# Router of a mixture-of-experts stage: fed from unscaled half rows, choices by the eight largest values, one load issued earlier

## The reference, cut to what matters

```python
h = x + merged @ w_out                         # 544 x 1024
xn = rms_norm(h, norm2_g)                      # h * rsqrt(mean(h*h) + EPS) * norm2_g
group_probs = softmax(xn @ w_group)            # 4 groups
gp, gi = top_k(group_probs, 1)
elog = (xn @ w_router).reshape(-1, 4, 8)       # 32 experts, 8 in each group
elog = take_along_axis(elog, gi)               # the 8 of the chosen group
ev, ei = top_k(elog, 2)
ew = softmax(ev) * gp
y = h + sum over the two chosen experts e of  ew * (silu(xn @ w_gate[e]) * (xn @ w_up[e])) @ w_down[e]
```

## Time and profile before

| | |
|---|---|
| median of 3 runs | 912.67 us (912.48 to 913.17) |
| profiled execution, device time | 908.81 us |
| its span, first to last instruction | 907.0 us |
| mean granted TensorE clock | 0.961 |
| PE busy | 822.3 us (91%) |
| DVE / ACT / POOL busy | 324.1 / 222.8 / 164.6 us |
| DMA, whole span | 164.65 MB, mean 182 GB/s |
| the chain that ended last, by engine | PE 72%, SP's queue 10%, DMA 6%, DVE 4% |

### The profile page before, as it was taken

How to read it: one execution, slowest core, us unless ns; L and a number is a source line. 1 busy time by engine, 2 the same in 40 slices (tenths; PEclk the granted TensorE clock), 3 DMA queues, 4 the chain that set the end, 5 groups by cost and what they waited for, 6 DMA issues and landing times.

```text
span 907.0 us, 11366 instructions
## 1 busy us (share of the span) xinstructions
PE 822.3 (91%) x4409; PEld 504.9 (56%) x4409; DVE 324.1 (36%) x882; ACT 222.8 (25%) x457; POOL 164.6 (18%) x225
## 2 busy tenths in 40 slices
PE   5989999999999989999999999996799999887860
PEld 3465444588665765676666684555455555454530
DVE  4222655998443531122222273545400000000005
ACT  3021332112333333333333430112122221111110
POOL 2323440000332222100000001100233232222110
PEclk9999999999999999999999999997799999999995
DMA  8523020421200200303021198217899999999968
GB/s 277 158 94 119 7 94 1 144 75 70 93 1 1 93 2 0 100 1 140 1 54 41 65 414 349 93 48 285 320 413 415 413 400 387 396 394 380 390 239 295
DMA packets 53159, 164.65 MB, mean 182 GB/s; under 512 B 13445, under 2 KB 15717, under 8 KB 44369
## 3 DMA queue, kind: packets, MB, share of 16 engines
q1 hardware_dynamic: 46432, 149.86, 43.9%
q0 software_dynamic: 6672, 14.06, 4.1%
HBM read 153.65 MB, written 18.08 MB: 189 GB/s over the span
## 4 chain that ended last, share of the span: by engine, by line
PE 72%; SPq 10%; DMA 6%; DVE 4%; POOL 3%; ACT 3%; issue 2%; POOLq 0%; DVEq 0%; ACTq 0%
PE quad L789 25%; PE pair L1120 9%; SPq L698 6%; PE pair L983 5%; PE quad L1339 4%; SPq L694 4%; PE pair L1339 4%; PE quad L857 3%; DMA arena<-in_w_up 3%; PE pair L1350 2%; PE pair L779 2%; PE quad L1077 2%; PE quad L1350 2%; POOL arena L1768 2%; PE pair L904 1%
## 5 line engine op out<-in xcount | busy, mean ns | idle before, releaser
L789 PE MATMUL quad<-ring_w,xnT 128*128 128x512 f32 (+1 forms) x192 | 79.4, 554 | 0.0
L983 PE MATMUL pair<-xnT,ring_w 128*128 128x272 f32 x256 | 70.2, 410 | 0.9 <-POOLq L1774 0.9
L1120 PE MATMUL pair<-xnT,ring_w 128*128 128x272 f32 x256 | 65.8, 403 | 0.0
L789 PE MATMUL quad<-xnT,ring_w 128*128 128x280 f32 (+1 forms) x256 | 60.6, 396 | 0.0
L1817 POOL DMA_INDIRECT ring_w<-xn_d,idx_x x32 | 32.7, 1022 | 131.4 <-PE quad L1332 63.2
L1339 PE MATMUL pair<-arena,ring_w 128*64 128x256 f32 x384 | 49.1, 414 | 7.6 <-DMA arena<-in_w_up 7.3
L983 PEld LDWEIGHTS pair<-xnT,ring_w 128*128 128x128 f32 x256 | 46.3, 192 | 16.7 <-issue 7.9
L1120 PEld LDWEIGHTS pair<-xnT,ring_w 128*128 128x128 f32 x256 | 46.6, 190 | 15.3 <-issue 6.9
L2057 DVE CUSTOM_DVE_ANT_0 arena<-quad,arena 128x528 f32<-128x528 f32 (+4 forms) x34 | 17.7, 521 | 103.9 <-PE quad L1175 60.9
L1339 PE MATMUL quad<-arena,ring_w 128*64 128x256 f32 x384 | 49.2, 414 | 6.2 <-DMA arena<-in_w_up 5.5
L789 PEld LDWEIGHTS quad<-xnT,ring_w 128*128 128x128 f32 x256 | 48.2, 190 | 11.2 <-issue 0.8
(11 more groups left out here) (267 smaller groups left out, 1237.7 us busy)
## 6 DMA issues: line engine op xcount, KB each, us to landing
arena<-in_w_gate SPq DMA_DIRECT2D x24, 1024.0 KB, 11.3
arena<-in_w_up SPq DMA_DIRECT2D x24, 1024.0 KB, 25.0
arena<-in_w_down SPq DMA_DIRECT2D x40, 512.0 KB, 13.7
ring_w<-in_w_in SPq DMA_DIRECT2D x8, 2048.0 KB, 8.5
ring_w<-in_w_down SPq DMA_DIRECT2D x20, 512.0 KB, 16.1
xnT<-in_w_gate SPq DMA_DIRECT2D x4, 1024.0 KB, 11.9
xnT<-in_w_up SPq DMA_DIRECT2D x4, 1024.0 KB, 24.8
hreg<-in_w_gate SPq DMA_DIRECT2D x4, 1024.0 KB, 11.0
```

The costliest lines, as they stand in the source:

```text
L789: last = nc.tensor.matmul(o, l, r, start=i == 0, stop=i == len(mms) - 1)
L983: last = nc.tensor.matmul(bank[6 + job % 2][:, 0:hi - lo], chunk8(6 + cb // 4)[:, k, c0:c0 + P], xT[:, k, lo:hi], start=k == 0, stop=k == ...
L1120: last = nc.tensor.matmul(bank[6 + job % 2][:, 0:hi - lo], w[:, k, c0:c0 + P], rhs[:, k, lo:hi], start=k == 0, stop=k == kt - 1)
```

## The change

- **Router on unscaled rows.** TensorE turns `h` itself (`X`), not the normed row. `norm2_g` is multiplied into `wr` beforehand: eight small loads on SP's queue at the start (`g2c`, 128 values each, one to a partition) and one GpSimd multiplication of 128x288. The factor `rstd` of a row changes neither the order of its logits nor the group; it is applied to the differences of logits at the end (two VectorE instructions on `gx`).
- **By half tiles.** A new semaphore `h_half` reports the first 512 columns. Squares, transposes and the router's product go by halves. The transposes, the router, the places and the entries are put between the matmuls of an output product (`output_part`); `places` and slots come one tile earlier.
- **Choices.** The eight largest values with their indices take the place of two rounds of maximum and compare; `marks` is reported ahead of `earlier` and of `gx`.
- **VectorE's order.** `second_norm(i-1)` and `choices(i-1)` now stand before `output_rows(i, 0)`. The weights `ew` are computed behind the slots of overflowing experts. The wait for the stored rows ahead of the indices is dropped; GpSimd's own stays.
- **Expert 5.** Its gate and up loads are issued once half 0 of the last tile is done (`pj_used[12]`), ahead of the store of the last tile's `h`.

```diff
-        J_B, J_WO, J_RT = 36, (52, 53, 56, 59, 62), (55, 58, 61, 64, 65)
+        J_B, J_WO, J_RT = 36, (52, 54, 57, 60, 63), (53, 56, 59, 62, 65)
...
+            for k in range(KT):
+                sp.dma_start(g2c[:, k:k + 1], a["norm2_g"][P * k:P * (k + 1)].rearrange("(p o) -> p o", o=1)).then_inc(g2c_in, 16)
...
             for i, t in enumerate(ORDER):
+                if i == NT - 1:
+                    sp.wait_ge(pj_ready, pj_used[12])
+                    load_gate_up(5, 5, gu_in[5])
                 sp.wait_ge(h_ready, i + 1)
...
             output_sample()
             for i in range(1, NT):
-                output_half(ORDER[i], 0)
-                x2_turned(i - 1)
-                if i >= 2:
-                    places(i - 2)
-                output_half(ORDER[i], 1)
-                routed(i - 1)
+                output_part(i, 0, 0, 2)
+                if i == 1:
+                    h_turned(0, 0)
+                h_turned(i - 1, 1)
+                output_part(i, 0, 2, 4)
                 if i >= 2:
                     entries(i - 2)
-            x2_turned(NT - 1)
-            routed(NT - 1)
-            for i in (NT - 2, NT - 1):
-                places(i)
-            for i in (NT - 2, NT - 1):
-                entries(i)
+                output_part(i, 0, 4, 6)
+                for h in range(2):
+                    routed(i - 1, h)
+                output_part(i, 0, 6, KT)
+                output_part(i, 1, 0, 4)
+                places(i - 1)
+                output_part(i, 1, 4, 6)
+                h_turned(i, 0)
+                output_part(i, 1, 6, KT)
+            entries(NT - 2)
+            routed(NT - 1, 0)
+            h_turned(NT - 1, 1)
+            routed(NT - 1, 1)
+            places(NT - 1)
+            entries(NT - 1)
...
+            row_squares(0, 0)
+            row_squares(0, 1)
+            h_columns(0, 0)
+            h_columns(0, 1)
+            for i in range(1, NT):
+                for h in range(2):
+                    row_squares(i, h)
+                    h_columns(i, h)
...
+            pool.wait_ge(wr_in, 32)
+            pool.wait_ge(g2c_in, 16 * KT)
+            link(nc.gpsimd.tensor_tensor(wr, wr, g2c.rearrange("p (k o) -> p k o", o=1).broadcast_to([P, KT, 36]),
+                                         ALU.mult))
...
+                link(nc.vector.max(tops[0:r, i, :], m))
+                link(nc.vector.max_index(top_at[0:r, :], tops[0:r, i, :], m))
+                link(nc.vector.tensor_copy(top_is[0:r], top_at[0:r, 0:2]))
+                tt(oh[0:r, :, i, :], iota[0:r, 0:NE].rearrange("p (c e) -> p c e", c=1).broadcast_to([r, 2, NE]),
+                   top_is[0:r].rearrange("p (c o) -> p c o", o=1).broadcast_to([r, 2, NE]), ALU.is_equal)
+                tt(marks[0:r, i, :], oh[0:r, 0, i, :], oh[0:r, 1, i, :], ALU.add)
+                nc.vector.sem_inc(marks_ready, 1)
...
+            for i in range(1, NT):
+                second_norm(i - 1)
+                choices(i - 1)
                 output_rows(i, 0)
+                nc.vector.sem_inc(h_half, 1)
+                row_ids(i - 1)
+                slots(i - 1)
+                output_rows(i, 1)
                 nc.vector.sem_inc(h_ready, 1)
+            second_norm(NT - 1)
             choices(NT - 1)
+            row_ids(NT - 1)
+            slots(NT - 1)
...
-            for t in (NT - 3, NT - 2):
-                dve.wait_ge(x2_stored[t], 16)
             dve.wait_ge(idx_part, NT)
             indices(idx_in, 0, NE)
```

More of the change, by code:

```diff
@@ L1246, in _, with output_part @@
             chunk_arrived(pe, 13)
[L1247 to L1251, removed]
+            pe.wait_ge(wr_ready, 1)
+            def output_part(i, c, k0, k1):
+                c0, n = columns(ORDER[i])[0][2], J_WO[i] + c
+                if k0 == 0:
+                    pj_wait_free(pe, n)
+                for k in range(k0, k1):
+                    last = nc.tensor.matmul(bank[n % 4], merged[:, k, c0:c0 + P], chunk8(12 + c)[:, k, :],
+                                            start=k == 0, stop=k == KT - 1)
+                if k1 == KT:
+                    last.then_inc(pj_ready, 1)
             def output_sample():
@@ L1262, in output_sample, with h_turned, routed @@
                 last.then_inc(pj_ready, 1)
-                pj[0] += 1
-            def x2_turned(i):
+            def h_turned(i, h):
                 r = TOK[ORDER[i]]
[L1267 to L1276, removed]
+                if h == 0:
+                    pe.wait_ge(h_half, i + 1)
+                else:
+                    pe.wait_ge(h_ready, i + 1)
+                x = X[0:r, ORDER[i], 512 * h:512 * (h + 1)]
+                tr_job([(x[:, P * j:P * (j + 1)], ident[0:r, 0:r]) for j in range(4)], r)
+            def routed(i, h):
+                r, n = TOK[ORDER[i]], J_RT[i]
+                pe.wait_ge(tr_free_act, emptied(TR, "act", T_X2 + 2 * i + h))
+                if h == 0:
+                    pj_wait_free(pe, n)
+                for k in range(4 * h, 4 * h + 4):
+                    last = nc.tensor.matmul(bank[n % 4][0:r, 0:36], x2T[:, i % 2, k, 0:r], wr[:, k, :], start=k == 0,
+                                            stop=k == KT - 1)
+                if h == 1:
+                    last.then_inc(pj_ready, 1)
             def places(i):
@@ L2135, in choices @@
                 dve.wait_ge(pj_ready, n + 1)
-                top, first, sel, m, e = v_max[0:r, i:i + 1], v_first[0:r], g_eq[0:r], masked[0:r], eq[0:r]
+                top, first, sel, m = v_max[0:r, i:i + 1], v_first[0:r], g_eq[0:r], masked[0:r]
                 red(top, lg[:, 0:NG], ALU.max)
@@ L2177, in _ @@
+            for v in (marks, earlier[:, 0, :], oh, gx, tops, rs2):
                 link(nc.vector.memset(v, 0.0))
```

151 lines of the change are left out of this document (73 added, 78 removed).

## The result

| | before | changed |
|---|---|---|
| first comparison, median | 912.40 us (6 runs) | 905.27 us (903.62 to 908.01, 6 runs) |
| ratio, 95% interval | | 0.9929 (0.9909 to 0.9949) |
| profiled execution, device time | 908.81 us | 905.41 us |
| its span | 907.0 us | 903.7 us |
| mean granted TensorE clock | 0.961 | 0.967 |

The two profiled executions stand only 3.4 us apart, while the medians stand 7.1 apart. So there are two questions: whether the traces' 3.4 to 3.6 us came about as forecast (2.5), and where the rest is.

A forecast was written before the change was run, and what follows sets the result against it. Bound by the experts' weight stream, so by expert 6's issue: later T0, shorter way to the gathers and less load beside them bring it 2.5 us sooner. Profiled 906.3 plus 3.9 carried over gives 910.2 us, range 906.8 to 912.9.

The forecast's parts named there:

- The frame: Stage of the experts: bound by the weight stream, so the end moves as expert 6's issue moves, microsecond for microsecond.
- T0: End of the last output product on TensorE: forecast 620.7, 4.6 us later than before.
- the stall in the first tile: TensorE waits in `h_turned(0,0)` for VectorE's add, which waits for the sample rows' DMA: 1.0 us.
- From T0 on the way: From T0 through `second_norm`, choices, slots and entries to the indices: ends at 632.3, T0 + 11.6; before it was 20.5.
- The store holds the gather: Last normed row's store, issued at 625.3 beside weights, lands after 7.9 us at 633.2; first gather starts at 633.3.
- rival 2: Store lands in turn with weights in 3 to 5 us, overlap free: expert 6 4.4 us sooner, 908.3; chance 0.20.
- The overlap of gathers and weights: Gathers meet 1 to 2 us of weights: 0.9 us added, expert 6 at 639.0 instead of 641.47.
- the last one: Final sum: profiled 906.3 us plus the 3.9 by which the median of before exceeded its profiled execution, giving 910.2.
- Case 1: Forecast itself: store and a short overlap hold the gathers, range 908.9 to 911.4 us; chance 0.45.
- Rival 3: Gathers take the loaded 6.9 us, so expert 6 goes as before: 912.7, half of it 911.5; chance 0.18.
- Rival 4: TensorE stalls in each of three tiles, no gain from 0.8 us a tile, 914.7 at 1.5; chance 0.09.
- rival 5: Eight small loads on SP's queue exceed their 15 us cover: caches 2.8 us late, 913.0; chance 0.02.

The follow-up runs named there:

- the store alone: Changed kernel, but SP waits for the landing of the last tile's normed row before issuing expert 4's weights: 906.87 us, ratio 0.9969.

## Why the prediction was right, and where it was wrong

**The frame was right.** The end moves as expert 6's issue moves: the rest is 265.3 to 266.1 us in all twelve traces, while that issue moves over 5.9 us.

**T0 was 1.4 too late.** Forecast 620.7, measured 619.3. T0 came 3.2 later than before (619.3 - 616.1). Of this 0.6 is the stall in the first tile (I had 1.0) and 0.16 a later front, so the moved work with its joins took 2.4 where I had 3.2 + 0.4. The durations that I added up have modelled ends that overlap the next operation: from start to start the four moved pieces of a tile take 1.70, 0.36, 0.44 and 0.36, 2.9 in all (TensorE's timeline), and the joins cost nothing. The last 0.4 I can't place. TensorE's timeline shows the stall, and the windows show no gap behind it (18.00 of 18):
```profile
552.88 0.68 PE L793 MATMUL pair<-cst,hreg 32*128 32x32 f32 x8 [0.59 <-DVEq L2236]
```
**From T0 on the way was forecast to a few tenths.** `second_norm` ends at T0 + 4.3 (forecast 4.3) and the choices begin at once. Their 11 instructions take 2.4 (2.7): the eight largest of 32 take 0.20, the search 0.09 + 0.18. The slots end at T0 + 8.9 (9.1). The indices are written at T0 + 10.6; a gather follows indices by 0.9 to 1.0, so it could have gone at T0 + 11.6, as forecast. Expert 5's gate went at 611.7 (612.7).

**The store holds the gather: right, for the landing too.** It was issued at T0 + 4.6 as forecast and took 7.88 (7.9, from the earlier trace rows). I let the gather start 0.1 behind the landing; GpSimd's release and the start of the instruction take 1.1. So 632.9 where I had 633.3: a T0 sooner by 1.4 and a start later by 1.0. The rule of the Trainium skill ("DMA: Bandwidth & Descriptors", section "Queues, rings and completion order") by which the queues are served in turn did not bring the store in sooner: it landed after 7.88 us and not after 3 to 5, so rival 2 did not come.

**The overlap of gathers and weights was over-priced.** I added 0.9 to 3.4; measured 3.6. The loads ran out between 635 and 636, where I had 636.0, but that is in part luck: they started 1.4 sooner than forecast (620.75) and ran about 1 us longer than the 13.9 that I gave them. The first gather met them for some 3 us and took 3.7. A likely reason that so little is lost is that a gather moves nothing at first: in the kernel before with expert 5 early, whose first gather starts at 636.94 with the engines empty, the DMA share is 0.00 until 638. No run tests it. Sum of the three: -1.4 + 1.0 - 0.7 = -1.1, which is 637.9 against 639.0.

**The step that failed is the last one**: "the median of before stands 3.9 above it, and I carry that over". Of the 4.9 us of the miss 3.9 are this and 1.0 comes from the terms above: by the profiled executions the forecast was 906.3 and the measurement 905.4. I took the offset of 3.9 for a fixed difference between a profiled execution and a timed one. There is none: in the eleven later traces the profiled execution is one of the timed ones and lies between 1.5 below and 3.0 above their median (904.27 against 905.72, 912.57 against 909.57). The runs show the 3.9 to be the gap between two levels on which executions of one and the same kernel fall. The three timed ones of before were all on the upper level and the profiled one on the lower; the changed kernel's runs are mostly on the lower. Three runs within 0.7 us said nothing of this, but the profiled execution did, outside their spread by 3.7: it should have been read as a second level, with both 906.3 and 910.2 within the range. The effect itself, 3.9 us on the lower level (ratio 0.9957), was forecast as 2.5.

**The rivals.** Case 1, the forecast itself, was the mechanism. Rival 3 (gathers beside weights) is what happens without the early load and with the store alone: 6.35 and 6.68 us for a gather. Rival 4 (stalls in each tile) and rival 5 (the small loads) did not come: no gap in the products, and the eight small loads hold SP's queue for 5.39 us of their cover of 15:
```profile
12.39 5.39 SPq L643 DMA_DIRECT2D small<-in_norm_g  x8
```
I had set the early load at 2 to 3 us; it was 3.1. The prediction does not see that it is worth nothing without the rest.

## What to carry to other kernels

When a path and the transfer that it runs into are of nearly the same length, shorten both or neither: here the early load alone gained nothing, the rest alone less than 1 us, and both together 3.9. Price a transfer by a row with the same traffic beside it (7.9 and not 3.0 for the same store), and ask what it delays when you clear its way. When the profiled execution lies outside the spread of the timed ones, take it as a second level of the kernel's time and put both into the range, not the difference onto the forecast. When two traces are compared, look first whether the granted clock fell equally often in them.

## What was not expected of the hardware

- A store of 0.5 MB from SBUF beside the stream of weights took 7.8 to 8.05 us to land in all ten traces that have it, issued by GpSimd (nine) or by SP (one). Without weights beside it, it landed within 3.05 (one trace).
- The first gather of 0.5 MB took 3.3 to 3.7 us where the weights were through or ran out within 3 us of its start, 4.7 with the store issued by SP, and 6.35 and 6.68 with weights beside it all the way.
- The granted clock fell to 1.2 GHz for some 3.5 us near 340 us in eight of twelve traces and not in the other four, and in one of them also at 296 us, after TensorE had been busy for 10.00 of 10 us. Each fall cost 1.7 us.
- Executions of one kernel fell on two levels 3 to 4 us apart, in shares that differed by session (5 of 6, 6 of 31, 15 of 34, 6 of 19 on the upper one). What decides between them is open; in the one traced execution of the upper level it was a second fall of the clock and a later start.
